# Running the last eight weight chunks of each down projection as two 256-token halves

## What is computed

```python
x = x + (jax.nn.silu(h @ w_gate[layer]) * (h @ w_up[layer])) @ w_down[layer]      # first block
...
def swiglu(x, w_gu, w_down):                                                     # second block
    g, u = jnp.split(x @ w_gu, 2, axis=-1)
    return (jax.nn.silu(g) * u) @ w_down
...
x = layer_norm(ALPHA * x + 0.5 * swiglu(x, ffn1_w_gu[l], ffn1_w_down[l]), ln1_g[l], ln1_b[l])
```

## Time and profile before

| | |
|---|---|
| time of the runs | 3522.5 us median, 3521.63 to 3523.46 |
| span of the profiled execution | 3520.6 us |
| its time less its span | the profile gives the span alone; the median of the runs is 1.9 us above it |
| instructions | 44495 |
| PE busy | 3484.5 us (99%), 15956 matmul records |
| PE weight loads | 2801.7 us (80%), 15956 records |
| VectorE, ScalarE, GpSimd busy | 1960.7, 1381.0, 465.3 us |
| mean DMA rate | 89 GB/s |
| mean granted TensorE clock | 0.998 |

### The profile page before, as it was taken

How to read it: one execution, slowest core, us unless ns; L and a number is a source line. 1 busy time by engine, 2 the same in 40 slices (tenths; PEclk the granted TensorE clock), 3 DMA queues, 4 the chain that set the end, 5 groups by cost and what they waited for, 6 DMA issues and landing times.

```text
span 3520.6 us, 44495 instructions
## 1 busy us (share of the span) xinstructions
PE 3484.5 (99%) x15956; PEld 2801.7 (80%) x15956; DVE 1960.7 (56%) x2532; ACT 1381.0 (39%) x1951; POOL 465.3 (13%) x321
## 2 busy tenths in 40 slices
PE   9999999999999999999999999999999999999998
PEld 6777888888777788888888876788878887678886
DVE  8888544425888644433543588533263327973324
ACT  5555433323555443323332366423243224662223
POOL 3333010001333110002100211100020003030002
PEclk9999999999999999999999999999999999999999
DMA  3112322223212222222322221222222222122222
GB/s 123 60 66 69 108 94 99 98 96 114 72 61 66 96 96 95 98 99 98 101 95 96 90 72 61 90 95 95 96 90 95 95 96 90 49 78 96 96 98 99
DMA packets 88241, 315.01 MB, mean 89 GB/s; under 512 B 10048, under 2 KB 10560, under 8 KB 87872
## 3 DMA queue, kind: packets, MB, share of 16 engines
q1 hardware_dynamic: 85824, 305.68, 25.9%
q10 hardware_dynamic: 2304, 7.80, 0.6%
HBM read 309.25 MB, written 4.19 MB: 89 GB/s over the span
## 4 chain that ended last, share of the span: by engine, by line
PE 83%; DVE 11%; DVEq 3%; ACT 2%; issue 1%; DMA 0%; SPq 0%; ACTq 0%
PE ps L1847 21%; PE ps L1848 20%; PE ps L1849 20%; PE sc L1847 5%; PE sc L1848 5%; PE sc L1849 5%; DVE w_lo L1121 3%; DVE cc_out L1703 2%; PE ps L2023 1%; DVE h_lo L1601 1%; ACT w_hi L542 1%; PE sc L2095 1%; DVEq L1459 1%; DVEq L1625 1%; PE ps L1946 0%
## 5 line engine op out<-in xcount | busy, mean ns | idle before, releaser
L1121 DVE TENSOR_TENSOR w_lo<-raw,w_hi 128x1024 fp32r<-128x1024 f32 x573 | 739.0, 1290 | 1110.4 <-ACT w_hi L542 1109.9
L542 ACT ACTIVATE w_hi<-raw 128x1024 fp32r<-128x1024 f32 x573 | 606.7, 1059 | 1412.8 <-PE ps L1849 757.2
L1847 PE MATMUL ps<-h_hi,w_hi 128*128 128x512 f32 x2576 | 1043.6, 405 | 9.3 <-DVE w_lo L1121 4.4
L1849 PE MATMUL ps<-h_hi,w_lo 128*128 128x512 f32 x2576 | 1005.4, 390 | 0.0
L1848 PE MATMUL ps<-h_lo,w_hi 128*128 128x512 f32 x2576 | 1004.4, 390 | 0.0
L1847 PEld LDWEIGHTS ps<-h_hi,w_hi 128*128 128x128 f32 x2576 | 484.5, 188 | 139.8 <-issue 40.1
L1849 PEld LDWEIGHTS ps<-h_hi,w_lo 128*128 128x128 f32 x2576 | 483.8, 188 | 103.2
L1848 PEld LDWEIGHTS ps<-h_lo,w_hi 128*128 128x128 f32 x2576 | 485.1, 188 | 92.7 <-issue 4.8
L1847 PE MATMUL ps<-hid_hi,w_hi 128*128 (+1 forms) x792 | 309.7, 391 | 0.0
L1849 PE MATMUL ps<-hid_hi,w_lo 128*128 (+1 forms) x792 | 308.2, 389 | 0.0
L1848 PE MATMUL ps<-hid_lo,w_hi 128*128 (+1 forms) x792 | 308.2, 389 | 0.0
(11 more groups left out here) (312 smaller groups left out, 4327.4 us busy)
## 6 DMA issues: line engine op xcount, KB each, us to landing
raw<-wts SPq DMA_DIRECT2D x573, 512.0 KB, 3.3
x<-xT ACTq DMA_DIRECT2D x1, 2048.0 KB, 7.9
parked<-x ACTq DMA_DIRECT2D x8, 256.0 KB, 2.0
x<-parked ACTq DMA_DIRECT2D x1, 2048.0 KB, 8.1
outT<-x SPq DMA_DIRECT2D x8, 256.0 KB, 2.1
x<-xT SPq DMA_DIRECT2D x5, 256.0 KB, 7.5
x<-xT ACTq DMA_DIRECT2D x3, 256.0 KB, 4.7
raw<-wts SPq DMA_DIRECT2D x2, 256.0 KB, 5.2
```

Source lines behind the costliest of these rows:

```text
L542: act(w_hi[:, s].rearrange("p a b -> p (a b)"), raw[:, s, :], ACT.Copy).then_inc(s_whi, 1)
L1121: tt(w_lo[:, s].rearrange("p a b -> p (a b)"), raw[:, s, :], w_hi[:, s].rearrange("p a b -> p (a b)").bitcast(F32), ALU.subtract).then_inc ...
L1847: mm(out, w_hi[:, s, b, :], hi, start=start, stop=False, skip_group_check=True)
L1849: return mm(out, w_lo[:, s, b, :], hi, start=False, stop=stop, skip_group_check=True)
```

## The change

The second loop of `down` gets one more level. A chunk's eight rows now run twice, once for the first 256 tokens and once for the last 256, each time with all 24 matmuls, on half the columns of the output bank and of the hidden rows. The weight tiles are the same in both halves and are loaded in each. `centre` moves to the second half, after four of its eight rows. The waits at the chunk's start and the signal at its end stay.

```diff
                 for i, n in enumerate(DOWN_ORDER):
                     s = i % 2
                     eng.wait_ge(s_wlo, pair0 * 2 + DOWN_ROWS + i + 3)
-                    for b in range(CHUNK):
-                        if centre and i == 2 and b == 6:
-                            centre()
-                        last = three(ps[n][:], s, b, hid_hi[:, DOWN_ROWS + b, :], hid_lo[:, DOWN_ROWS + b, :], False,
-                                     b == CHUNK - 1)
+                    for c in range(0, SEQ, SEQ // 2):
+                        for b in range(CHUNK):
+                            if centre and i == 2 and c and b == 4:
+                                centre()
+                            r = DOWN_ROWS + b
+                            last = three(ps[n][:, c:c + SEQ // 2], s, b, hid_hi[:, r, c:c + SEQ // 2],
+                                         hid_lo[:, r, c:c + SEQ // 2], False, b == CHUNK - 1)
                     last.then_inc(s_used, 1)
```

## The result

The changed kernel takes **3533.1 us** (median of 7 runs, 3533.00 to 3533.23) against 3522.5 (7 runs beside it, 3521.50 to 3523.46): ratio 1.0031, 95% interval 1.0020 to 1.0042. It is slower by 10.6 us, which is 0.3%. The forecast was 3524.8 us, within 0.2% of no change, with a chance of 0.60 for that. The range, 3518.5 to 3540.0, holds the time; the likeliest case did not come about.

What follows compares the result with a forecast made beforehand. TensorE's gapless matmul steps were taken as the bound: 2304 halves x 114.35 = 263.5 us replace 261.1, +2.3 us; 3520.6 + 2.3 + 1.9 (median above profiled span) = 3524.8 us, range 3518.5 to 3540.

Steps and rivals of the forecast that it cites:

- likeliest case: Down projections: 256-column halves step at 114.4 ns, +2.3 us in all, 3524.8 us; chance 0.52.
- rival 4: TensorE's instruction supply in the tails: instructions arrive too slowly, one 2.8 us stall per tail, 3542 us; chance 0.05.
- rival 3: Weight loads in the down projections don't overlap running matmuls: 224 ns per half, +255 us; chance 0.02.
- c = 114.4 ns: Step of each 256-column half in the down projections, taking the 11.4 ns loss to go with the columns; +2.3 us.
- three rows: Profile evidence for a column-borne loss: 166 ns 4-column record, 0.39 us matmul before a load pause, 0.43 us half-clock steps.
- rival 1: Every down-projection half: the 11.4 ns loss goes with the instruction, 120.1 ns per half, +15.6 us, 3538.1 us; chance 0.18.
- 4-column record: Folded norm's 4-column matmul, 166 ns: no room for 11 ns more, so the loss was taken to go with columns.
- matmul before a pause: Last matmul before loads pause 2.7 us still takes 0.39 us, so the 11 ns aren't the price of a load beside it.
- At granted clock 0.50 the loss vanishes: Two fp32r matmuls at 2129.0 to 2132.2 us start 0.43 us apart; read as operands arriving at about 2.28 columns per ns.
- a load fits into 112 ns: Weight load of each down-projection half: hides below the 114.4 ns step with 2 ns to spare.
- The rest costs nothing: Outside the matmul steps, centring-sum wait, weight-buffer release, ScalarE and VectorE: no cost found and no gain.
- Rival 2: Down-projection halves: load enters the path or halves never settle, 117.5 ns each, +9.6 us, 3532.1 us; chance 0.12.

Runs made afterwards that it cites:

- the sweep: Chunks of all six tails cut in two at 480, 448, 416, 352, 320, 288, 272 and 256 columns, against the kernel before: 3575.44 us, ratio 1.0152.
- 384 + 128: The change with parts of 384 and 128 columns instead of two of 256; 3585.82 us, ratio 1.0181 against the kernel before.
- late-chunks kernel: Halves only in the last four chunks of the second block's four centred tails, against the kernel before: 3523.24 us, ratio 1.0003.
- repeated weights: The change with both halves of a matmul adjacent, loading the same weight tile twice in a row; 3533.33 us, ratio 1.0033 against the kernel before.

## Why the prediction was wrong in its likeliest case

**The bound was read rightly.** TensorE's own steps set the pace: the runs follow the sum of steps in each part, less what the waits behind it give back, to a few tenths of a us.

**The counts and the form of the sum held.** 1152 more matmuls, tails from first to last as many steps as said, the clock unchanged, nothing lost to instruction fetching (rival 4: no tail has a gap that it didn't have before) and loads that go on beside running matmuls (rival 3: the step is 120.0 ns, not 224, each with a load of its own that starts with the running matmul, both at 790.05 in the first tail).

**The step that failed is the choice of c = 114.4 ns**, "because three rows speak for a loss that goes with the columns". It measured 120.0, which is rival 1's value of 120.1. Taking 5.7 ns too few, 2304 times, is 13.0 us. Each of the three rows was read rightly and none showed what I drew from it:

- The 4-column record has no 11 ns in it. The sweep shows why this says nothing of wide matmuls: records of up to 128 columns show at most 4 ns, the settled ones from 256 on 10 to 15. (The 0 at 4 columns is there by construction, since the 164.3 were read off that record.) A point at 4 columns can't be joined by a line to one at 512.
- The matmul before a pause still takes 0.39 us. That speaks against the load running beside it, as far as a record goes whose end is modelled, and the plain fp32 matmuls speak against it more strongly; but it tells nothing of columns against instruction.
- At granted clock 0.50 the loss vanishes: 0.43 us from start to start, where 512 columns at 1.2 per ns are 426.7 ns. I had noted that a fixed cost could hide behind a slow array too. The later trace shows the same with 448 columns (below). It doesn't decide.

I had one wide size only, 512, and no second point; the chance of 0.18 for rival 1 was too low for what the rows could tell.

**The cover for the load was right**: "a load fits into 112 ns" became 111.6 to 111.8 in eight widths. At 256 columns, with steps of 120.0 ns, the load isn't the bound. It is for 240 and less, and that made 384 + 128 cost six times as much as 256 + 256.

**"The rest costs nothing" missed a gain.** My step said that no due time moves, since a chunk is hardly longer. With 13.3 ns per split a chunk lasts 0.32 us more, and in the second block VectorE uses the last four to catch up: 4.1 us come back, of 15.7. The rows for it, the waits for `w_lo` behind each centred tail, were in the trace before; I had looked at the tails and not at the seam behind them. Rival 1 as written (+15.6, 3538.1 us) is therefore right in its mechanism and too slow by 5 us. Rival 2's 3532.1 lies nearer to the measured time by accident: its sign, 277 ns records at 117.5 ns steps, didn't appear.

No version here beats the kernel before. The late-chunks kernel can't be told from it (+0.03%), since of the 5.5 us that it adds to its tails 4.2 lie in time that TensorE waited anyway.

## What to carry to other kernels

Price a split of a matmul from two wide sizes, not from one wide and one tiny: for fp32r on this chip, in this kernel, each matmul of 256 to 512 columns costs its columns plus 12 to 16 ns, and a run of 24 narrower ones, each with a 128x128 load of its own, settles at 111.6 to 111.8 ns per matmul and not below. So use the full bank width wherever nothing is gained by finishing a half sooner. When the bounding engine is made slower, look at the next wait behind the changed stretch: as much comes back as the helper engine was late, if the delay lies where that engine works without a pause, and none of it if the delay lies where it waits.

## What was not expected of the hardware

In the sweep TensorE's granted clock fell to 0.50 for 3.4 us in two of six tails, a microsecond after the part of 32 columns, that is 24 matmuls that start 0.11 us apart. In the four other tails the same part was followed by no fall, and no other run has one in a tail; that the narrow matmuls caused it is a guess. The rows give the stretches before, during and after, and two matmuls in it:

```profile
1994.20:1999.00 4.80, 4.80 (x35) 4.54 (x34) 0.62 (x1) 0.64 (x1) 0.00 (x0) 1.00 0.27 102
1999.20:2002.60 3.40, 3.40 (x10) 3.00 (x10) 1.23 (x1) 0.22 (x1) 0.00 (x0) 0.50 0.20 72
2002.60:2005.00 2.40, 2.40 (x15) 2.20 (x13) 0.00 (x0) 0.00 (x0) 0.00 (x0) 1.00 0.29 116
...
2000.39 0.57 PE L1849 MATMUL ps<-hid_hi,w_lo 128*128 128x448 f32 x1
2000.76 0.57 PE L1847 MATMUL ps<-hid_hi,w_hi 128*128 128x448 f32 x1
```

PE shows as busy the whole time, since records overlap; only the clock column tells. It cost about 1.6 us in each of those tails: their down projections are 10.76 us longer than before, the other two centred ones 9.16. Inside, 448 columns step at 373.3 ns, which is 448 / 1.2 to the digit: at granted clock 0.50 the fixed cost, 16.2 ns at this width in the table, is gone. Whatever it is, something that runs beside the array's columns would look so; no run shows it. What it is stays open. The plain fp32 rows speak against the load of the next weights, and the repeated weights against a change of weights and, for one step against two, against the distance between additions into one PSUM address.
